# At least three product pieces in a row between groups of small matmuls in TensorE's planned order

## The reference

```python
proj = h @ w_in
y_a = deltanet_branch(...) @ w_up_dn
y_b = swa_sink_branch(...) @ w_up_sw
mix = (sigmoid(gate_a) * y_a + sigmoid(gate_b) * y_b) @ w_o
x = x + rmsnorm(mix, post_mix_g)
ff = jnp.square(jax.nn.relu(h2 @ w_ff1)) @ w_ff2
# in the delta rule, for each head and chunk of the sequence:
u = triangular_solve(L, v * beta); w = triangular_solve(L, kb * exp(g))
v_new = u_c - w_c @ state
o = qd @ state + a_c @ v_new
state = state * exp(gl) + kd.T @ v_new
```

## Time and profile before

| | |
|---|---|
| median of 3 runs | 2476.6 us (2475.43 to 2478.47) |
| the profiled execution's own time | 2473.5 us |
| its span | 2471.7 us |
| TensorE busy, share of the span | 97% |
| VectorE, ScalarE, GpSimd busy | 50%, 43%, 47% |
| mean granted clock of TensorE | 0.987 |

### The profile page before, as it was taken

One profiled execution on the slowest core, in us unless ns is written; L12 is line 12 of the kernel. 1 busy time (PEld: TensorE's weight loads), 2 busy tenths in 40 slices (PEclk: granted clock), 3 DMA queues, 4 the chain that ended last, 5 costly groups with the idle time before them and its releaser, 6 DMA issues.

```text
span 2471.7 us, 35072 instructions
## 1 busy us (share of the span) xinstructions
PE 2401.6 (97%) x13972; PEld 1909.9 (77%) x13972; DVE 1229.9 (50%) x2140; ACT 1069.4 (43%) x2281; POOL 1149.4 (47%) x848
## 2 busy tenths in 40 slices
PE   7999999999999999989999999999999999899998
PEld 5787777777778888867878777777778788777876
DVE  4777854673441111177767546733486611465153
ACT  5566643543343223245655434433442332434442
POOL 4333323334666556543333333346665554543454
PEclk9999999999999999999999999999999999989999
DMA  3211111222222233222111121223224333364322
GB/s 140 69 52 48 56 52 60 61 77 77 94 77 94 94 95 99 93 70 64 52 45 61 44 69 60 77 78 103 77 86 142 114 112 94 100 174 136 94 94 77
DMA packets 76516, 207.48 MB, mean 84 GB/s; under 512 B 16705, under 2 KB 27713, under 8 KB 75841
## 3 DMA queue, kind: packets, MB, share of 16 engines
q1 hardware_dynamic: 76352, 205.24, 26.5%
HBM read 194.72 MB, written 10.49 MB: 83 GB/s over the span
## 4 chain that ended last, share of the span: by engine, by line
PE 84%; DVE 8%; ACT 4%; POOL 2%; issue 1%; DMA 0%; SPq 0%; DVEq 0%; ACTq 0%; POOLq 0%
PE ps L966 24%; PE ps L968 22%; PE ps L967 22%; PE ps L1901 2%; PE ps L1905 2%; PE ps L1954 1%; PE ps L1966 1%; PE ps L1882 1%; ACT wH L922 1%; POOL wL L929 1%; PE ps L1960 1%; DVE ctw L1176 1%; ACT prob L1439 1%; DVE ctmp L1176 1%; PE ps L1931 1%
## 5 line engine op out<-in xcount | busy, mean ns | idle before, releaser
L929 POOL TENSOR_TENSOR wL<-raw,wH 128x512 fp32r<-128x512 f32 x660 | 897.9, 1381 | 1127.1 <-ACT wH L922 1126.9
L922 ACT ACTIVATE wH<-raw 128x512 fp32r<-128x512 f32 x660 | 379.8, 623 | 757.3 <-PE ps L968 753.3
L966 PE MATMUL ps<-hH,wH 128*128 128x512 f32 x1592 | 664.3, 417 | 1.7 <-POOL wL L929 1.7
L968 PE MATMUL ps<-hH,wL 128*128 128x512 f32 x1592 | 628.8, 395 | 0.0
L967 PE MATMUL ps<-hL,wH 128*128 128x512 f32 x1592 | 627.3, 394 | 0.0
L966 PEld LDWEIGHTS ps<-hH,wH 128*128 128x128 f32 x1592 | 301.2, 189 | 71.6 <-issue 8.7
L968 PEld LDWEIGHTS ps<-hH,wL 128*128 128x128 f32 x1592 | 300.6, 189 | 67.0
L967 PEld LDWEIGHTS ps<-hL,wH 128*128 128x128 f32 x1592 | 302.0, 190 | 52.3 <-issue 0.5
L966 PE MATMUL ps<-OH,wH 128*128 128x512 f32 x576 | 230.8, 401 | 5.0 <-DVE acc L1761 1.8
L968 PE MATMUL ps<-OH,wL 128*128 128x512 f32 x576 | 227.8, 396 | 0.0
L967 PE MATMUL ps<-OL,wH 128*128 128x512 f32 x576 | 227.8, 395 | 0.0
(11 more groups left out here) (406 smaller groups left out, 3438.4 us busy)
## 6 DMA issues: line engine op xcount, KB each, us to landing
raw<-w SPq DMA_DIRECT2D x345, 512.0 KB, 3.5
mats<-matsD SPq DMA_DIRECT2D x4, 1408.0 KB, 6.7
x<-xT SPq DMA_DIRECT2D x8, 256.0 KB, 5.9
matsD<-Cd SPq DMA_DIRECT2D x8, 256.0 KB, 2.8
matsD<-wide SPq DMA_DIRECT2D x4, 512.0 KB, 3.6
mats<-lagsD SPq DMA_DIRECT2D x32, 64.0 KB, 6.3
outT<-acc SPq DMA_DIRECT2D x8, 256.0 KB, 2.2
matsD<-tab SPq DMA_DIRECT2D x8, 128.0 KB, 1.8
```

The costliest lines, as they stand in the source:

```text
L922: act.activation(weights_at(slot)[0][:, k, :], raw[:, n % RAW, k, :], ACT.Copy).then_inc(high_done, 1)
L929: pool.tensor_tensor(low[:, k, :], raw[:, n % RAW, k, :], high[:, k, :].bitcast(F32), ALU.subtract).then_inc(low_done, 1)
L966: pe.matmul(out, wh, rH[:, t, :], start=(t == 0), stop=False)
L968: mm = pe.matmul(out, wl, rH[:, t, :], start=False, stop=(t == depth - 1))
```

## The change

The planner `ordered` gets a rule. It remembers as `since` the planned start of the first product piece of the present run of pieces. While a run is on, a step of TensorE that is not a piece may start no earlier than `RUN` = 3.0 pieces after `since`, and 0.1 is added to its start. Once a small step is taken, `since` is empty, and further small steps and the first next piece are free of the rule. The changed starts are also those that the planner goes on with. Both blocks use the rule; no instruction is added or removed, only the order on each engine is made anew.

```diff
-def ordered(chains, needs, engine_of, micros, hop):
+RUN, CHANGE = 3.0, 0.1
+
+
+def ordered(chains, needs, engine_of, micros, hop, piece=5.12 / PARTS):
     heads = [0] * len(chains)
+    since = None
...
             start = max([free.get(engine_of(e), 0.0)] + [ended[b] + hop for b in before])
+            if engine_of(e) == "pe" and e[0] != "mm" and since is not None:
+                start = max(start, since + RUN * piece) + CHANGE
             if best is None or start < best[0] - 1e-9:
                 best = (start, n, e)
         start, n, e = best
+        if engine_of(e) == "pe" and (e[0] == "mm") != (since is not None):
+            since = start if e[0] == "mm" else None
         free[engine_of(e)] = ended[e] = start + micros(e)
```

## The result

The changed kernel takes 2547.45 us (median of 4 runs, 2546.34 to 2548.46) against 2476.96 us before: a ratio of 1.0275, 95% interval 1.026 to 1.029, so 70.5 us more. The profiled execution has a span of 2544.7 us, 73.0 more than before. I had forecast slower, by 20 us, and my slowest case ended at 2538 us; the sign and the place were right, the size was not.

What follows compares the result with a forecast made beforehand. TensorE, 97% busy, bounds the kernel. Switches -11, uncovered steps and ends +28, clock +3 make +20 us on 2476.6: 2496.6 us. Forecast's own range 2482 to 2518, whole range 2463 to 2538.

Steps and rivals of the forecast that it cites:

- my slowest case: Upper end of the whole range: much slower, with its own spread, 2538 us.
- The place and the mechanism: In the heads, the delayed chain of small inverse steps holds up evacuations, so TensorE waits with no product allowed.
- 62 A steps: Inverse steps in the heads covered by 216 product pieces at 3.5 each; about 87 must be through before swq2.
- the bar: At swq2, perhaps a tile or more earlier: products wait for small chains, 25 inverse steps planned without products beside them.
- The later bar at piece 7 of ya0: Products there wait for head 7's recurrence; with swq6's bar, some 7 more inverse steps without products.
- The weight splits: On ScalarE and POOL, moved with the small steps; costed at nothing because POOL has slack in the heads.
- The term of the clock: In the heads, one clock fall of 7 us in all costs 3 us; between none and two a layer, 0 to 12.
- The term of the uncovered steps: In the heads, inverse steps without products plus recurrence ends: 14 us idle a layer, 28 in two; 3 to 30 a layer.
- the ends of B: Recurrence ends of heads 5, 6 and 7, where products wait: 2 us each, 6 us; 5.2 each if uncovered.
- The term of the switches: Heads, windows and second block: fewer switches between products and small matmuls gain 11 us, between 5 and 20.
- The Trainium skill's rule: TensorE pulling weight loads ahead would hide switches, leaving no saving and a sum 11 us higher; the prediction kept the saving.
- Rival 2: Heads and windows: early, frequent product waits, two clock falls a layer; idle 27, clock 5 a layer; +53, 2530 us; chance 0.12.

Runs made afterwards that it cites:

- the pauses: Kernel before with six TensorE pauses in the MLP, each waiting for two or five VectorE operations: 2498.23 us (1.0077) and 2517.46 us (1.0161).
- A free: Changed kernel with the steps of the heads' inverse exempt from the rule: 2471.17 us (0.9962), in more rounds 2470.50 us (0.9961).
- A and C free: Changed kernel with the steps of the heads' inverse and of the windows exempt from the rule: 2477.26 us (0.9994).

## Why the prediction was wrong

**The place and the mechanism were right.** The bound, products in a fixed order against a chain of thirteen steps a head, held as the prediction put it: I took 62 A steps covered by products before the bar; on the chip 64 (heads 0 to 3 and twelve of head 4) stand before the hole at swq1. The bar fell a tile before swq2, through D of head 7. Freeing A removed the loss, putting A alone under the rule kept 70% of it. The later bar at piece 7 of ya0 is there too. The weight splits, put at nothing, cost nothing: TensorE's waits for `wL` and `xwL` are 2.5 us before and 0.5 us after.

**The term of the clock failed.** I took one fall in all, 3 us, and bound it by two a layer, 12 us in all. There are three in the first layer's heads and four in the second's, 68 us at the lower level, and over the program 66.0 us more than before, in 46.5 of which TensorE was busy: 20.9 us by the price that the pauses and the earlier trace rows give. The price for each us was right, and the number and length of the falls were not. My row showed a fall after a single short gap, but I read the holes as stretches in which TensorE still did small matmuls. Windows before and within the first layer's falls:

```profile
335.00:341.00 6.00, 3.45 (x60) 2.75 (x58) 3.88 (x12) 4.51 (x14) 0.00 (x0) 1.00 0.01 3
...
342.00:355.00 13.00, 9.96 (x57) 7.70 (x54) 4.66 (x12) 3.23 (x8) 1.58 (x2) 0.50 0.00 0
...
376.00:382.00 6.00, 3.77 (x22) 2.96 (x21) 2.06 (x4) 1.80 (x4) 1.26 (x1) 0.50 0.00 0
...
451.00:460.00 9.00, 4.76 (x13) 3.59 (x14) 5.18 (x10) 2.17 (x5) 2.46 (x2) 0.50 0.00 0
```

The first fall begins at 341.4 us. The longest wait in the hole up to then was 1.19 us; the wait of 2.57 us comes after it (timeline below). So a row of short waits was enough here. Amid products, pauses of 2.0 us brought a fall two times in six.

**The term of the uncovered steps was little over half of what came.** Forecast 28 us of idle, measured 50.8. I reckoned 25 steps at 1.45 us before swq2, seven more at the later bars, and 0.25 us of idle in each. Measured: 38.1 us from the first small matmul of the hole to the first product for 18 A steps, 2.1 us a step, with 7.7 us of idle (39.00 - 31.29), 0.43 us a step. I had p to q and q to p from a stretch in which A ran freely. In the hole TensorE's one order holds A, B and D, and it waits for whichever is next in it, the longest wait being 2.57 us for `qd` on GpSimd, a step of D:

```profile
336.41 0.65 PE L1892 MATMUL ps<-cst,vs 128*128 128x128 f32 x4 [0.90 <-ACT kd L1396]
...
338.87 0.66 PE L1933 MATMUL ps<-cst,osq 128*128 128x128 f32 x4 [1.19 <-DVE osq L1630]
...
339.89 0.66 PE L1913 MATMUL ps<-XB,Pm 64*64 64x32 f32 x16
341.60 0.63 PE L1901 MATMUL ps<-cst,XB 64*64 64x64 f32 x4 [1.05 <-DVE XB L1604]
344.80 1.44 PE L1890 MATMUL ps<-ks 128*128 128x128 f32 x5 [2.57 <-POOL qd L1313]
```

A D step's matmuls behind that wait run at the lower clock. The stretch from 361 to 379 us adds 4.5 us of idle (18.00 - 13.46). And the ends of B were dearer than the 2 us each that I took: the window from 444 to 457 us has 7.5 us of idle, where I took 2 for each end and 5.2 at most: 2.91 + 2.85 us are the end proper, before turno and before the last piece, and the rest lies in the chain of B's steps, which I had reckoned as covered. Over the layer it is 612.00 - 584.13 = 27.9 us of idle, against 580.00 - 575.71 = 4.3 in the same stretch before (first row), so +23.6, within the bound of 30 and far from the 14 that I chose:

```profile
60.00:640.00 580.00, 575.71 (x4129) 452.86 (x4128) 361.76 (x714) 289.35 (x711) 216.55 (x159) 1.00 0.20 63
...
60.00:672.00 612.00, 584.13 (x4120) 462.68 (x4119) 376.75 (x714) 289.93 (x710) 214.99 (x158) 0.97 0.19 59
1160.00:1770.00 610.00, 580.72 (x4089) 461.16 (x4087) 354.13 (x687) 280.91 (x694) 216.42 (x159) 0.97 0.19 59
```

**The term of the switches was too high.** Forecast -11 us. In the changed kernel the rest in the table is +1.3, a saving and the ends of the new waits together, so it can't be read off there. I expected 73 fewer groups a layer and got 55 and 61, because groups in which no A step was ready came as often as I feared. In the kernels without holes 69 fewer groups (A free) go with -2.8 us and 67 fewer (A and C free) with -0.6, 0.04 and 0.01 us each in place of my 0.07, in single profiles. No saving came from the second block (-0.4 us between its start and end piece by piece, nothing to be told when it has the rule alone).

The Trainium skill's rule that weight loads are pulled ahead of matmuls in flight ("TensorE: Matmul & The Clock Gate", section "Architectural detail"), taken to hide a switch, would leave the kernel with A free as it was before; it is 0.4% faster. But the one with A and C free has nearly as many groups fewer and is no faster, so these runs don't settle it; the edges in the earlier trace rows stay as measured.

**The range.** Rival 2 (idle 27 us a layer, clock 5 a layer, 2530) came nearest. Its idle was close to the 50.8 measured, though not by its count: it took 54 steps as covered, and 64 were. Its clock was half of what came. With the measured terms the sum is 50.8 (idle) + 20.9 (clock) + 1.3 (the rest) = +73.0. My range left that out, because I bounded the clock by two falls a layer without a row on how readily it falls. Even the high ends of both terms with the smallest saving, 60 + 12 - 5 = +67, would have ended at 2544 us.

## What to carry to other kernels

A rule that makes a shared engine's small steps wait for a batch is paid by the longest serial chain through that engine: count its steps, multiply by the batch, and compare with the filler work that exists before the first consumer of the chain. If the chain needs more, exempt it and batch the others: here that turned a loss of 2.8% into a gain of 0.4%. And price each new hole twice, once as waiting and once in the clock that the work behind it gets.

## What the runs showed of the hardware

The granted clock of TensorE falls more readily than I had expected. Amid dense products it fell after every pause of 4.1 us and after two of six pauses of 2.0 us. In the heads it fell at 341.4 us, amid small matmuls between which TensorE had waited 1.19 us at most since the hole began at 322.3 us. At the lower level TensorE took 0.46 us more for each us in which it was busy there (9.0 us for 19.7, long against short pauses, mostly products). The time at the lower level is no measure of the loss by itself: of the 66.0 us more in the changed kernel TensorE was busy in 46.5. Added product matmuls in the hole cost more than they gave: 22.8 us of them for 15.3 us less at the lower level.
